# Second layer of a two-layer hybrid backbone: keys, values, queries and one convolution chunk projected ahead of the two gate chunks

## The chip, the cores and the metric

One core of one Trainium2 chip. The metric is the device time of one launch in microseconds (us); lower is better. Every time below is of the kernel as it stands, from three timed runs and one profiled execution.

## What is computed

The reference runs two layers over 256 latent tokens and 256 context tokens of width 1024. Each layer projects its normalised input with one matrix `w_in`, whose columns feed three parallel groups of heads, and then applies an output projection and a SwiGLU. Cut to what matters here:

```
proj  = h  @ p['w_in']                       # latent tokens: all columns
projc = hc @ p['w_in'][:, :n_ctx_cols]       # context, last layer: keys, values, xb and dt alone
xb = silu(dwconv(proj[xb]));  cm = silu(dwconv(proj[C]))      # state-space heads
y  = ssd_scan(xb, dt, a, bm, cm, init) + ssd_d * xs           # both directions
y_ssd = rmsnorm(y * silu(z))                                  # z: the gates
q = rope(rmsnorm(q)); k = rope(rmsnorm(k)); y_att = rmsnorm(softmax(q k') v)
y_hy  = rmsnorm(x0 * long_conv(v * x1))                       # hy: dwconv of 6 chunks
x = x + g1 * (concat(y_ssd, y_att, y_hy) @ w_out)
```

All arithmetic is float32; every product with a weight is three matmuls, of a rounded and a rest part of each side.

## The kernel before

The four instruction streams (SP for loads, TensorE, ScalarE, VectorE) are written by hand, each as a Python loop; each runs in the order in which it is written, with semaphores between them. A weight passes as pieces of 128x1024 elements through a ring of four buffers (`RING`). SP loads piece i once piece i-4 has been used (`w_used`), ScalarE rounds it (`round_w`, L1305), VectorE takes the rest (`split_w`, L1689), TensorE multiplies.

The stage "in" has 15 chunks of 256 columns, two pieces each, so 30 pieces. The list `W_IN` (L42) sets their order for both layers: four `xbc` chunks (state-space inputs), two `z` (the gates), `kv` (keys and values), two `q` (queries), six `hy` (convolution). I call piece s of the stage slot s. Work beside the projections is hung on slots by the constants of L79 to L82: in slot s TensorE runs `at_piece(s)`, then half of the piece's matmuls, then `in_piece(s)`, then the other half. In the second layer this is

- slots 7, 8, 9: transposes of x and B; slot 11 (`S_G`): the products of B and C
- slots 12 to 20 (`S_HEAD`): one state-space head a slot. TensorE spreads the sums (`cum_rows`, L805, L807), ScalarE exponentiates (L1433), VectorE adds and masks (L1947, L1948), and in the next slot TensorE makes the head's output (L818), which VectorE adds to `ysum` (L1877)
- slots 13 to 24 (`S_STATE`): the states, all through one PSUM bank `ACC` that the head outputs share. TensorE fills it in `in_piece` (L908, L914) once VectorE has read what was in it (`acc_read`)
- slots 18 to 24: queries and keys are squared (`S_SQUARES`, L1449, sums at L1974), scaled by their roots (`S_ROOTS` 20, L1460) and turned by the rotary tables (`S_ROPE` 21 to 24, L2006 to L2019), and TensorE transposes the outcome from slot 23 on (`S_TURN`)
- slots 25 to 27 (`S_GATE`): `ysum` times the silu of z, its root mean square (`token_rms`, L1288 to L1290), its scaling; slot 29 (`S_FEAT`): transposed and split (L1695)

A chunk is read out of PSUM in the even slot after it: `kv` and `q` by VectorE (L1855, L1861), `z` by ScalarE (L1378, Silu), `hy` by both (L1373, then L1838 and L1842). Two pairs of banks take turns; a `q` or `z` chunk takes both, so the chunk behind it waits until it is read out (`pair_open`).

ScalarE needs a function table for Silu and one for Ln and Exp. `preload_act_table_set("natural_log_exp_and_others")` at slot `S_HEAD` (L1425) loads one set that has Ln and Exp both. Where the program holds no such call, the build puts an `ACT_TABLE_LOAD` ahead of an activation whose function the loaded set lacks. In the stage "out" behind it, Ln and Exp come in pairs: `norm_features` for the convolution (`hrs`, ahead of the softmaxes) and for the attention (`ars`, behind them), then `norm` (L1262, L1263) ahead of the SwiGLU. The next preload is that of Silu, at L1582.

Of the kernel before, what the change touches and what calls it, by code (L numbers as in the profile page):

```python
# [30 lines left out]
CW = 256  # L31
OFF_K, OFF_XB, OFF_DT, OFF_C, OFF_Q, OFF_Z, OFF_HY = 0, 256, 1024, 1040, 1296, 1808, 2320
# [6 lines left out]
NV = NA + NB  # L39


W_IN = ([("xbc", OFF_XB + CW * i, i) for i in range(3)] + [("xbc", OFF_C, 3)]  # L42
        + [("z", OFF_Z + CW * i, i) for i in range(2)] + [("kv", OFF_K, 0)]
        + [("q", OFF_Q + CW * i, i) for i in range(2)]
        + [("hy", OFF_HY + CW * i, i) for i in (0, 2, 1, 3, 4, 5)])

FFN = [(0, 6), (6, 5)]
DOWN_ROWS = [(0, 4, 8, 12), (0, 4, 7, 10)]
# [29 lines left out]

S_DT, S_CUMS, S_XS0, S_XS1, S_B, S_G, S_HEAD, S_STATE, S_GATE, S_FEAT = 5, 6, 7, 8, 9, 11, 12, 13, 25, 29  # L79

S_SQUARES, S_ROOTS, S_ROPE, S_TURN = 18, 20, 21, 23
S_FOLD, S_TABLES = (24, 27), (20, 15)  # L82

S_TAPS, S_SUMS, S_SPEC = 6, 8, 9
# [1 line left out]
V_SINE0, V_SINE1, V_TAPS = 6, 9, 12  # L86

SMALL_LOADS, LATE_LOADS = 14, 5
CONV_CHUNKS = sum(kind in ("xbc", "hy") for kind, _, _ in W_IN)
FEAT_BANK = ((5, 6, 7, 5), (5, 6, 7, 4))  # L90


# [107 lines left out]
def backbone(nc, x, c, ctx_in, c_ctx, w_mod, b_mod, norm1_g, w_in, ssd_conv_w, ssd_conv_b, ssd_a_log,  # L200
# [3 lines left out]
    with ExitStack() as stack:  # L204
# [18 lines left out]
        xbc = at("xbc", 88, [8, T])  # L223
# [185 lines left out]
        def _(sp):  # L409
# [52 lines left out]

            def load_in(l, s):
                ch, half = in_source(s)
                kind, col, idx = W_IN[ch]
                if kind in ("z", "q"):

                    i, k0 = PLAN[l, "in"][0] + s, 4 * idx + 2 * (s % 2)
                    if i >= RING:
                        sp.wait_ge(w_used, i - RING + 1)  # L470
                    c0 = col - CW * idx
                    sp.dma_start(w_raw[:, i % RING, :].rearrange("p (k n) -> p k n", n=2 * CW),
                                 w_in[l].rearrange("(k p) n -> p k n", p=P)[:, k0:k0 + 2, c0:c0 + 2 * CW]).then_inc(w_full[i % RING], 16)
# [28 lines left out]
            for l in range(DEPTH):  # L502
# [66 lines left out]
        def _(pe):  # L569
# [169 lines left out]
            for l in range(DEPTH):  # L739
# [488 lines left out]
        def _(act):  # L1228
# [89 lines left out]
            for l in range(DEPTH):  # L1318
# [30 lines left out]
                for s in range(2, 32):  # L1349
# [4 lines left out]
                        round_w(g0 + 4)  # L1354
                        round_w(g0 + 5)
                    if ch >= 0 and s % 2 == 0:
                        kind, _, idx = W_IN[ch]
                        q = q0 + ch
                        b = 2 * (q % 2)
                        if kind in ("xbc", "hy"):  # L1360
                            act.wait_ge(w_used, g0 + max(2 * ch + 2, 4))
                            if kind == "hy" and idx == 3:
                                p.after("hyv_ready")
                            for jj in range(2):
                                blk = 2 * idx + jj
                                if kind == "xbc":
                                    wide = T if idx < 3 else n
                                    dst, wc, bc = xbc[:, blk, 0:wide], V_SCW + 8 + blk, V_SCB + blk
                                else:
                                    wide = n  # L1370
                                    dst = x1t[:, jj, 0:n] if idx in (2, 3) else (hyv, None, x0)[idx // 2][:, blk % 4, 0:n]
                                    wc, bc = V_HCW + 12 + blk, V_HCB + blk
                                A(dst, ps[:, b + jj, 0:wide], ACT.Identity, scale=vecT[:, l, wc:wc + 1],  # L1373
                                  bias=vecT[:, l, bc:bc + 1]).then_inc(conv_init, 1)
                        if kind == "z" and idx == 1:
                            act.wait_ge(w_used, g0 + 2 * ch + 2)
                            for t in range(tiles):
                                ins = A(zs[:, t, :], ps[:, 2 * ((q - 1 + t // 2) % 2) + t % 2, :], ACT.Silu)  # L1378
                                if t % 2 == 1:
                                    ins.then_inc(pair_free[(q - 1 + t // 2) % 2], 1)  # L1380
                                elif tiles == 2:
                                    ins.then_inc(pair_free[q % 2], 1)
                    if 4 <= s < 30:
                        round_w(g0 + s + 2)
                    if s % 2 == 1 and s >= 3 and W_IN[(s - 3) // 2][0] == "xbc":
                        q, idx = q0 + (s - 3) // 2, W_IN[(s - 3) // 2][2]
                        wide = T if idx < 3 else n
                        act.wait_ge(pair_free[q % 2], q // 2 + 1)
                        p.sig(A(xbc[:, 2 * idx:2 * idx + 2, 0:wide], xbc[:, 2 * idx:2 * idx + 2, 0:wide], ACT.Silu), "conv_ready")
# [46 lines left out]
                    if s == S_HEAD:  # L1436
# [2 lines left out]
                            hd = slice(h * HD, (h + 1) * HD)  # L1439
                            ins = A(ysum[:, 0:tiles, hd], xsn[:, 0:tiles, hd], ACT.Copy, scale=bc16[:, l, 2, h:h + 1])  # L1440
                        p.sig(ins, "ysum_init")
                    if s in (S_SQUARES, S_SQUARES + 1):
                        if s == S_SQUARES:
                            p.after("qk_ready")
                        for t in (2 * (s - S_SQUARES), 2 * (s - S_SQUARES) + 1):
                            if t >= 2:
                                p.after("head_ss")
                            h0 = 0 if t < tiles else 512
                            p.sig(A(hsqs[:, t % 2, h0:QKW], qk[:, t, h0:QKW], ACT.Square), "heads_squared")  # L1449
                    if s == S_HEAD + HEADS + 1:  # L1450
                        p.after("y_head_done", 2)
                    if s == S_ROOTS:
                        p.after("head_ss", 2)
                        p.chain(A(rs40[:], rs40[:], ACT.Ln, scale=1.0 / HD, bias=eps1[:, 0:1]))
                        p.chain(A(rs40[:], rs40[:], ACT.Exp, scale=-0.5))
                    if S_ROOTS <= s < S_ROOTS + 4:
                        t = s - S_ROOTS
                        for h in range(0 if t < tiles else 8, 10):
                            qh = qk[:, t, h * HD:(h + 1) * HD]
                            ins = A(qh, qh, ACT.Copy, scale=rs40[:, t, h:h + 1])  # L1460
                        p.sig(ins, "heads_scaled")
# [165 lines left out]
        def _(dve):  # L1627
# [147 lines left out]
            for l in range(DEPTH):  # L1775
# [35 lines left out]
                for s in range(2, 32):  # L1811
# [5 lines left out]
                        p.after("dt_psum")  # L1817
                        p.sig(V.tensor_copy(csT[0:32, :], ps[0:32, 6, :]), "dt_rows")
                    if ch >= 0 and s % 2 == 0:
                        kind, _, idx = W_IN[ch]  # L1820
                        q = q0 + ch
                        b = 2 * (q % 2)
                        if kind in ("xbc", "hy"):
# [125 lines left out]
                    if state_at(s) is not None:  # L1949
# [16 lines left out]
                            p.chain(TT(heads(ps[:, ACC, :]), heads(ps[:, ACC, :]), per_head(ecs, reader, d), ALU.mult))  # L1966
                            p.sig(TT(ysum[:, reader, :], ysum[:, reader, :], ps[:, ACC, :], ALU.add), "acc_read")
                        split_w(g0 + s + 2)
                    if s in (S_SQUARES, S_SQUARES + 1):
                        for t in (2 * (s - S_SQUARES), 2 * (s - S_SQUARES) + 1):  # L1970
                            h0 = 0 if t < tiles else 8
                            p.after("heads_squared")
                            p.own("qk_ready")
# [2 lines left out]
                    if s == S_TABLES[l]:  # L1976
# [342 lines left out]
```

## Time and profile before

| | |
|---|---|
| median of three runs | 1304.5 us (1302.06 to 1306.15) |
| the profiled execution | 1304.85 us |
| its span, first to last instruction | 1303.0 us, mean granted TensorE clock 0.992 |
| TensorE busy | 1241.6 us (95%) |
| VectorE busy | 700.9 us (54%) |
| ScalarE busy | 524.0 us (40%) |
| DMA | 131 GB/s over the span |

The profile gives for each engine the time in which it executed something, and for each idle stretch what ended it. Start times count from the first instruction. Instructions on one engine overlap a little (the next starts before the one ahead has ended), so what an instruction costs its queue is the distance from its start to the next one's start.

### The profile page before, as it was taken

Reading aid. Unit: us, or ns where it says so; the run is one execution under the profiler, and the core shown is the slowest. Engines: PE = TensorE matmul, PEld = TensorE weight load, DVE = VectorE, ACT = ScalarE, POOL = GpSimd, SP = SyncE. Lnnn points to the kernel's source line nnn. Section 1 sums busy time; section 2 is a strip of 40 time slices with the busy share of each in tenths; the row PEclk is TensorE's granted clock in tenths of the full one; section 3 lists DMA queues with packets and bytes.
Section 4 is the critical chain, followed back from the end, with each engine's and each line's share of the span. In section 5 each row is a group of like instructions: output and inputs, shape, how many; then the busy total and the mean of one; then the engine's idle time right before and its main releaser. Section 6 shows DMA issues by size and latency. Waiting matters only on the chain. (4 is left out here: it accounts for less than half of the span.)

```text
span 1303.0 us, 17960 instructions
## 1 busy us (share of the span) xinstructions
PE 1241.6 (95%) x7476; PEld 994.5 (76%) x7476; DVE 700.9 (54%) x1193; ACT 524.0 (40%) x902; POOL 1.7 (0%) x8
## 2 busy tenths in 40 slices
PE   5899999999999899999999999999998898999998
PEld 3566777777676677677777788768878677999998
DVE  1645256877866643432232333465479877555554
ACT  4443434542444433222112222246555354543444
POOL 0000000000000000000000000000000000000000
PEclk9899999999999999999999999999999999999999
DMA  9632344441112264455445322313334213555553
GB/s 362 216 131 97 98 145 137 139 146 49 33 39 92 65 217 150 147 177 178 162 177 178 128 93 83 107 43 95 106 98 130 90 34 98 184 188 178 183 178 126
DMA packets 129256, 171.90 MB, mean 132 GB/s; under 512 B 9204, under 2 KB 112278, under 8 KB 128152
## 3 DMA queue, kind: packets, MB, share of 16 engines
q1 hardware_dynamic: 128692, 170.58, 39.6%
q8 instruction: 59, 0.97, 0.3%
q10 hardware_dynamic: 484, 0.18, 0.1%
q14 instruction: 21, 0.17, 0.0%
HBM read 169.69 MB, written 1.05 MB: 131 GB/s over the span
## 5 line engine op out<-in xcount | busy, mean ns | idle before, releaser
L1689 DVE TENSOR_TENSOR w_lo<-w_raw,w_hi 128x1024 fp32r<-128x1024 f32 (+1 forms) x220 | 264.1, 1203 | 313.0 <-ACT w_hi L1305 312.5
L1305 ACT ACTIVATE w_hi<-w_raw 128x1024 fp32r<-128x1024 f32 (+1 forms) x220 | 228.4, 1042 | 386.3 <-DMA w_raw<-in_w_gu_dram 182.2
L654 PE MATMUL ps<-h_hi,w_hi 128*128 128x512 f32 (+1 forms) x896 | 311.9, 348 | 3.8 <-ACT gate L1597 1.8
L656 PE MATMUL ps<-h_hi,w_lo 128*128 128x512 f32 (+1 forms) x896 | 304.1, 339 | 0.0
L655 PE MATMUL ps<-h_lo,w_hi 128*128 128x512 f32 (+1 forms) x896 | 304.1, 339 | 0.0
L654 PEld LDWEIGHTS ps<-h_hi,w_hi 128*128 128x128 f32 x896 | 170.8, 191 | 38.0 <-issue 20.3
L654 PE MATMUL ps<-f_hi,w_hi 128*128 128x512 f32 (+1 forms) x544 | 187.8, 345 | 5.7 <-DVE att_lo L2205 2.7
L656 PEld LDWEIGHTS ps<-h_hi,w_lo 128*128 128x128 f32 x896 | 170.8, 191 | 19.1
L655 PEld LDWEIGHTS ps<-h_lo,w_hi 128*128 128x128 f32 x896 | 171.0, 191 | 16.9
L656 PE MATMUL ps<-f_hi,w_lo 128*128 128x512 f32 (+1 forms) x544 | 182.9, 336 | 0.0
L655 PE MATMUL ps<-f_lo,w_hi 128*128 128x512 f32 (+1 forms) x416 | 139.9, 336 | 0.0
L654 PEld LDWEIGHTS ps<-f_hi,w_hi 128*128 128x128 f32 x544 | 103.1, 190 | 23.5 <-issue 6.8
L656 PEld LDWEIGHTS ps<-f_hi,w_lo 128*128 128x128 f32 x544 | 103.1, 190 | 10.9
L655 PEld LDWEIGHTS ps<-f_lo,w_hi 128*128 128x128 f32 x416 | 78.9, 190 | 8.3 <-issue 0.5
L705 PE MATMUL ps<-h_hi,w_hi 128*128 128x512 f32 (+1 forms) x128 | 48.9, 382 | 10.8 <-DVE h_lo L1641 5.3
L2223 DVE TENSOR_TENSOR hidden<-gate,ps 128x1024 f32<-128x1024 f32 (+1 forms) x22 | 20.9, 952 | 55.7 <-PE ps L656 55.5
L706 PE MATMUL ps<-h_lo,w_hi 128*128 128x512 f32 (+1 forms) x128 | 48.3, 377 | 0.0
L707 PE MATMUL ps<-h_hi,w_lo 128*128 128x512 f32 (+1 forms) x128 | 48.0, 375 | 0.0
L1488 ACT ACTIVATE prob<-ps,sm 128x512 f32<-128x512 f32 (+1 forms) x48 | 29.1, 611 | 40.5 <-DVE sm L2098 38.0
L966 PE MATMUL ps<-w_hi,h_hi 128*128 128x512 f32 x96 | 40.5, 421 | 0.0
L705 PEld LDWEIGHTS ps<-h_hi,w_hi 128*128 128x128 f32 x128 | 25.5, 199 | 16.9 <-issue 10.7
L1433 ACT ACTIVATE em<-ps,bia 128x128 f32<-128x128 f32 x96 | 26.5, 381 | 27.9 <-PE ps L807 27.9
(301 smaller groups left out, 1580.1 us busy)
## 6 DMA issues: line engine op xcount, KB each, us to landing
w_raw<-in_w_gu_dram SPq DMA_DIRECT2D x88, 512.0 KB, 3.6
w_raw<-in_w_in_dram SPq DMA_DIRECT2D x60, 512.0 KB, 3.7
m_raw<-in_w_mod_dram SPq DMA_DIRECT2D x32, 512.0 KB, 4.7
w_raw<-in_w_down_dram SPq DMA_DIRECT2D x32, 512.0 KB, 3.4
m_even<-in_w_mod_dram SPq DMA_DIRECT2D x12, 1024.0 KB, 5.8
m_odd<-in_w_mod_dram SPq DMA_DIRECT2D x12, 1024.0 KB, 5.8
m_first<-in_w_mod_dram SPq DMA_DIRECT2D x8, 1024.0 KB, 10.8
w_raw<-in_w_out_dram SPq DMA_DIRECT2D x16, 512.0 KB, 3.4
```

The source lines that it names most:

```text
L654: mm(o, w_hi[:, i % RING, w], hi[:, 0:n], start=first and k == 0, stop=False)
L655: mm(o, w_hi[:, i % RING, w], lo[:, 0:n], start=False, stop=False)
L656: last = mm(o, w_lo[:, i % RING, w], hi[:, 0:n], start=False, stop=final and k == nk - 1)
L705: mm(o, w_hi[:, s, w], hi, start=(half == 0 and k == 0), stop=False)
L706: mm(o, w_hi[:, s, w], lo, start=False, stop=False)
L707: last = mm(o, w_lo[:, s, w], hi, start=False, stop=(half == 1 and k == 3))
L966: mm(o, h_hi[:, b, tok], w_hi[:, (i + half) % RING, w], start=(b == 0), stop=False)
L1305: A(w_hi[:, i % RING, w], w_raw[:, i % RING, w], ACT.Copy).then_inc(w_hi_done, 1)
L1433: ins = A(em[:, 2 * (h % 2) + d, t * P:(t + 1) * P], ps[:, 6 + d, t * P:(t + 1) * P], ACT.Exp, bias=bia[:, t, d * 8 + h:d * 8 + h + 1])
L1488: p.sig(A(prob[:, i % 2, j, 0:keys], ps[:, 4 + j, 0:keys], ACT.Exp, bias=sm[:, 0, c:c + 1], accum_out=sm[:, 1, c:c + 1]), "probs_ready")
L1689: TT(w_lo[:, i % RING, w], w_raw[:, i % RING, w], w_hi[:, i % RING, w].bitcast(F32), ALU.subtract).then_inc(w_lo_done, 1)
L2223: TT(hidden[:, :, 0:n], gate[:, :, 0:n], ps[:, 2 * ((q + 1) % 2):2 * ((q + 1) % 2) + 2, 0:n], ALU.mult).then_inc(pair_free[(q + 1) % 2], 1)
```

## The change

The list is now one per layer. The first layer's is the old one. In the second layer the old chunks 4 and 5 (the gates) come after the old chunk 9: four `xbc`, `kv`, two `q`, `hy` 0, two `z`, then the other five `hy`. With it the squares (slots 14, 15), the roots (slots 16 to 19) and the first two rotary steps (slots 17, 18) move forward in the second layer; the last two rotary steps stay at 23 and 24, and so do the transposes, the gate and all state-space work.

```
-W_IN = ([("xbc", OFF_XB + CW * i, i) for i in range(3)] + [("xbc", OFF_C, 3)]
-        + [("z", OFF_Z + CW * i, i) for i in range(2)] + [("kv", OFF_K, 0)]
-        + [("q", OFF_Q + CW * i, i) for i in range(2)]
-        + [("hy", OFF_HY + CW * i, i) for i in (0, 2, 1, 3, 4, 5)])
+W_IN_0 = ([("xbc", OFF_XB + CW * i, i) for i in range(3)] + [("xbc", OFF_C, 3)]
+          + [("z", OFF_Z + CW * i, i) for i in range(2)] + [("kv", OFF_K, 0)]
+          + [("q", OFF_Q + CW * i, i) for i in range(2)]
+          + [("hy", OFF_HY + CW * i, i) for i in (0, 2, 1, 3, 4, 5)])
+W_IN = [W_IN_0, [W_IN_0[i] for i in (0, 1, 2, 3, 6, 7, 8, 9, 4, 5, 10, 11, 12, 13, 14)]]
...
-S_SQUARES, S_ROOTS, S_ROPE, S_TURN = 18, 20, 21, 23
+S_SQUARES, S_ROOTS, S_ROPE, S_TURN = (18, 14), (20, 16), ((21, 22, 23, 24), (17, 18, 23, 24)), 23
...
-                    if S_ROOTS <= s < S_ROOTS + 4:
-                        t = s - S_ROOTS
+                    if S_ROOTS[l] <= s < S_ROOTS[l] + 4:
+                        t = s - S_ROOTS[l]
...
-                    if S_ROPE <= s < S_ROPE + 4:
-                        t = s - S_ROPE
+                    if s in S_ROPE[l]:
+                        t = S_ROPE[l].index(s)
```

The rest of the diff puts `W_IN[l]` for `W_IN` and `S_SQUARES[l]` for `S_SQUARES`. Line numbers of the changed kernel are one higher than those of the one before.

VectorE in slots 17 and 18 of the second layer, before (em, ysum and st are the state-space heads' tiles, w_lo the rest of a weight piece):

```order
L1877 TENSOR_TENSOR ysum<-ysum,ps 128x2x64
L1947 TENSOR_TENSOR em<-em 128x256
L1948 TENSOR_TENSOR em<-em,gT 128x256
L1955 TENSOR_TENSOR st<-st,etot 128x512
L1960 TENSOR_TENSOR st<-st,ps 128x512
L1937 TENSOR_TENSOR xw<-xsn,wst 128x512
L1689 TENSOR_TENSOR w_lo<-w_raw,w_hi 128x1024
L1861 COPY qk<-ps 128x512 x2
L1868 MEMSET rs_119 128x40
L1877 TENSOR_TENSOR ysum<-ysum,ps 128x2x64
```

The same place of the change, from slot 17's state on to the head output's addition in slot 18 (hbuf and ropt are the rotary tiles):

```order
L1956 TENSOR_TENSOR st<-st,etot 128x512
L1961 TENSOR_TENSOR st<-st,ps 128x512
L1938 TENSOR_TENSOR xw<-xsn,wst 128x512
L1690 TENSOR_TENSOR w_lo<-w_raw,w_hi 128x1024
L2007 TENSOR_TENSOR hbuf<-qk,gcos_92 128x128
L2013 TENSOR_TENSOR ropt<-qk,gsin_94 128x2x16 x4
L2007 TENSOR_TENSOR hbuf<-qk,gcos_92 128x4x64
L2013 TENSOR_TENSOR ropt<-qk,gsin_94 128x4x16 x4
L2007 TENSOR_TENSOR hbuf<-qk,gcos_92 128x4x64
L2013 TENSOR_TENSOR ropt<-qk,gsin_94 128x4x16 x4
L2020 TENSOR_TENSOR hbuf<-hbuf,ropt 128x128
L2020 TENSOR_TENSOR hbuf<-hbuf,ropt 128x4x64 x2
L1878 TENSOR_TENSOR ysum<-ysum,ps 128x2x64
```

A whole rotary step now stands between the state of slot 17 and the addition of slot 18, and a second one behind the state of slot 18; before, the read-out of the queries stood there.

ScalarE from the second layer's root mean square of `ysum` (slot 26) on, before:

```order
L1288 ACTIVATE xsn,st_117<-ysum 128x512 x2
L1289 ACTIVATE st_117<-st_117,eps_104 128x2
L1290 ACTIVATE st_117<-st_117 128x2
L1305 ACTIVATE w_hi<-w_raw 128x1024
L1373 ACTIVATE x_62<-ps,vecT 128x256 x2
```

and in the change:

```order
L1289 ACTIVATE xsn,st_117<-ysum 128x512 x2
L1290 ACT_TABLE_LOAD
L1290 ACTIVATE st_117<-st_117,eps_104 128x2
L1291 ACT_TABLE_LOAD
L1291 ACTIVATE st_117<-st_117 128x2
L1306 ACTIVATE w_hi<-w_raw 128x1024
L1374 ACTIVATE x_62<-ps,vecT 128x256 x2
```

The read-out of the gates (Silu) now comes behind the preload of slot 12, with a table load of its own ahead of it, and nothing loads the common set of Ln and Exp again: each Ln and each Exp behind it has a load. In the same way `hrs`, `ars` (L1502, L1503) and the norm's `lnt`, `rstd` (L1263, L1264) have a load each, so the second layer has nine table loads more than before: one for the gates and two for each of the four Ln and Exp pairs.

## Rows read from the trace of the kernel before

**Rows 1.** Windows: from:to, length, busy of PE, PEld, DVE, ACT, POOL, clock, DMA share, GB/s
```profile
909.13:937.74 28.61, 27.98 (x186) 24.84 (x184) 13.46 (x19) 16.96 (x33) 0.00 (x0) 1.00 0.32 95
937.74:1013.10 75.36, 66.15 (x445) 59.00 (x445) 65.42 (x155) 42.28 (x98) 0.00 (x0) 0.98 0.40 119
955.00:965.00 10.00, 8.54 (x51) 7.35 (x50) 7.33 (x13) 4.67 (x11) 0.00 (x0) 0.83 0.21 58
```

**Rows 2.** Waits of PE, 937.74 to 1013.10: us in total, times, longest us
```profile
PE ps L886 <- DVE hbuf L2019: 2.3, 2, 2.0
PE ps L914 <- DVE ysum L1877: 1.5, 2, 1.2
PE ps L914 <- DVE st L1960: 1.5, 1, 1.5
PE ps L654 <- DVE qk L1861: 1.5, 1, 1.5
```

**Rows 3.** Timeline of PE: start us, us, instruction, idle before it
```profile
909.13 1.04 PE L861 MATMUL ps<-c_sq,xbc 128*128 128x128 f32 x8
...
937.74 0.39 PE L805 MATMUL ps<-csr,pick 40*128 40x256 f32 x2
...
958.08 0.36 PE L654 MATMUL ps<-h_hi,w_hi 128*128 128x256 f32 x1 [1.46 <-DVE qk L1861]
...
1013.10 0.63 PE L1018 MATMUL ps<-c_sq,v_even 128*128 128x128 f32 x4 [1.47 <-DVE f_lo L1695]
```

**Rows 4.** Timeline of DVE, slots 17 to 22
```profile
953.56 0.68 DVE L1955 TENSOR_TENSOR st<-st,etot 128x512 f32<-128x512 f32 x1
954.31 0.69 DVE L1960 TENSOR_TENSOR st<-st,ps 128x512 f32<-128x512 f32 x1
954.91 0.69 DVE L1937 TENSOR_TENSOR xw<-xsn,wst 128x512 f32<-128x512 f32 x1
955.51 1.22 DVE L1689 TENSOR_TENSOR w_lo<-w_raw,w_hi 128x1024 fp32r<-128x1024 f32 x1
956.65 1.28 DVE L1861 COPY qk<-ps 128x512 f32<-128x512 f32 x2
...
964.63 1.54 DVE L1974 TENSOR_REDUCE rs<-hsqs 128x10 f32<-128x640 f32 x2
...
979.26 0.29 DVE L2006 TENSOR_TENSOR hbuf<-qk,gcos 128x128 f32<-128x128 f32 x1
...
982.62 0.87 DVE L1838 SCALAR_TENSOR_TENSOR x1t<-ps,vecT,x1t 128x255 f32<-128x255 f32 x2
```

**Rows 5.** Timeline of ACT, slots 7 and 20
```profile
903.83 1.04 ACT L1305 ACTIVATE w_hi<-w_raw 128x1024 fp32r<-128x1024 f32 x1
904.89 1.28 ACT L1389 ACT_TABLE_LOAD   x1
906.18 1.06 ACT L1389 ACTIVATE xbc<-xbc 128x1024 f32<-128x1024 f32 x1
...
971.49 2.49 ACT L1460 ACTIVATE qk<-qk,rs 128x64 f32<-128x64 f32 x10
```

**Rows 6.** Timeline of ACT, second layer's stage "out"
```profile
1038.62 0.47 ACT L1501 ACTIVATE hrs<-ps,eps 128x256 f32<-128x256 f32 x1 [1.22 <-PE ps L1128]
...
1040.41 0.69 ACT L1488 ACTIVATE prob<-ps,sm 128x512 f32<-128x512 f32 x1 [0.87 <-DVE sm L2098]
...
1076.40 0.47 ACT L1501 ACTIVATE ars<-ps,eps 128x256 f32<-128x256 f32 x1 [1.33 <-PE ps L1146]
...
1098.20 0.47 ACT L1262 ACTIVATE lnt<-ps,eps 128x256 f32<-128x256 f32 x1 [0.79 <-PE ps L680]
1098.70 0.42 ACT L1263 ACTIVATE rstd<-lnt 128x256 f32<-128x256 f32 x1
```

**Rows 7.** Waits of PE, 1013.1 to 1102
```profile
PE ps L705 <- DVE h_lo L1641: 2.8, 1, 2.8
...
PE ps L654 <- DVE att_lo L2205: 1.0, 1, 1.0
PE ps L680 <- ACT sqr L1255: 0.9, 1, 0.9
```

More of the change, by code:

```diff
@@ L88 @@
 SMALL_LOADS, LATE_LOADS = 14, 5
-CONV_CHUNKS = sum(kind in ("xbc", "hy") for kind, _, _ in W_IN)
+CONV_CHUNKS = sum(kind in ("xbc", "hy") for kind, _, _ in W_IN[0])
 FEAT_BANK = ((5, 6, 7, 5), (5, 6, 7, 4))
@@ L464, in load_in @@
                 ch, half = in_source(s)
-                kind, col, idx = W_IN[ch]
+                kind, col, idx = W_IN[l][ch]
                 if kind in ("z", "q"):
@@ L932, in _ @@
                 step_sizes()
-                for ch, (kind, col, idx) in enumerate(W_IN):
+                for ch, (kind, col, idx) in enumerate(W_IN[l]):
                     if ch < 2:
@@ L1356, in _ @@
                     if ch >= 0 and s % 2 == 0:
-                        kind, _, idx = W_IN[ch]
+                        kind, _, idx = W_IN[l][ch]
                         q = q0 + ch
@@ L1384, in _ @@
                         round_w(g0 + s + 2)
-                    if s % 2 == 1 and s >= 3 and W_IN[(s - 3) // 2][0] == "xbc":
-                        q, idx = q0 + (s - 3) // 2, W_IN[(s - 3) // 2][2]
+                    if s % 2 == 1 and s >= 3 and W_IN[l][(s - 3) // 2][0] == "xbc":
+                        q, idx = q0 + (s - 3) // 2, W_IN[l][(s - 3) // 2][2]
                         wide = T if idx < 3 else n
@@ L1441, in _ @@
                         p.sig(ins, "ysum_init")
-                    if s in (S_SQUARES, S_SQUARES + 1):
-                        if s == S_SQUARES:
+                    if s in (S_SQUARES[l], S_SQUARES[l] + 1):
+                        if s == S_SQUARES[l]:
                             p.after("qk_ready")
-                        for t in (2 * (s - S_SQUARES), 2 * (s - S_SQUARES) + 1):
+                        for t in (2 * (s - S_SQUARES[l]), 2 * (s - S_SQUARES[l]) + 1):
                             if t >= 2:
@@ L1451, in _ @@
                         p.after("y_head_done", 2)
-                    if s == S_ROOTS:
+                    if s == S_ROOTS[l]:
                         p.after("head_ss", 2)
@@ L1819, in _ @@
                     if ch >= 0 and s % 2 == 0:
-                        kind, _, idx = W_IN[ch]
+                        kind, _, idx = W_IN[l][ch]
                         q = q0 + ch
@@ L1968, in _ @@
                         split_w(g0 + s + 2)
-                    if s in (S_SQUARES, S_SQUARES + 1):
-                        for t in (2 * (s - S_SQUARES), 2 * (s - S_SQUARES) + 1):
+                    if s in (S_SQUARES[l], S_SQUARES[l] + 1):
+                        for t in (2 * (s - S_SQUARES[l]), 2 * (s - S_SQUARES[l]) + 1):
                             h0 = 0 if t < tiles else 8
```

## The prediction

> **What bounds the kernel now.** The page's first part comes first: TensorE is busy for 95% of the span, so only its idle time and its slow time can be won or lost. The windows then show where these lie in the stage that changes. Slots 8 to 13 (909.13 to 937.74) are TensorE's: 27.98 us busy of 28.61, with VectorE busy for 13.46 [rows 1]. From slot 14 to the first matmul of the stage behind it (937.74 to 1013.10) TensorE is busy for 66.15 us of 75.36, VectorE for 65.42 [rows 1, 3]. Two engines with equal work that hand results to each other set this stretch. TensorE idles 9.2 us in it. The waits name VectorE every time: 2.3 for the rotary tile hbuf, 1.5 and 1.5 for the bank that the states share, 1.5 for the read-out of the queries [rows 2], 1.47 for f_lo at the end [rows 3]. From 955 to 965 the granted clock is 0.83 [rows 1], close behind the 1.46 us wait of slot 18 [rows 3]. Part of that time is at 1.2 instead of 2.4 GHz, about 10 x 0.17 = 1.7 us lost.
>
> **Slots 8 to 13.** Before they hold four z pieces and two kv pieces, now two kv and four q pieces. A q piece has the matmuls of a z piece, and the transposes and first heads stay in their slots. The sum is unchanged, so slot 14 starts about 28.6 us behind slot 8 as before [rows 3]. **0.0 us**. The pieces behind kv load while the first q pieces run, as they did before; ScalarE needs the first of them 6 us earlier than TensorE, and that slack stays.
>
> **Slots 14 to the end of the stage.** TensorE has the same matmuls in another order. VectorE has 1.3 us less (the kv read-out, now in slot 10). So nothing is removed here; the question is where the waits fall. I laid out both queues from slot 14's start, each instruction at its distance in the rows: a weight rest 1.14 (955.51 to 956.65), the state's two steps and the weighing 0.75 + 0.60 + 0.60, a rotary step 3.36 (979.26 to 982.62), the two sums of squares 1.5, the q read-out 1.3 to 1.4 [rows 4], ten scaled copies on ScalarE 2.49 [rows 5].
> - Slot 14: hy 0 waits until VectorE has read q. The second head's exponentials now come late, since slots 12 and 13 are short (3.4 and 5.1 us) and ScalarE spends 1.28 on a table, 2.4 on ysum and two weight roundings ahead of them. VectorE so ends its slot 13 work about 2.5 after slot 14's start, and the read-out at 3.9. TensorE is there at 1.2 and waits 2.7; before, 1.46.
> - Slots 15 and 16: the sums of squares, the tables and hy 0's convolution put VectorE some 2 us behind, and ScalarE's scaling (2.49) holds back the exponentials of slot 17. TensorE waits about 1.2 in all.
> - Slot 18: TensorE stands at the state matmul at 23.8. The bank is free only when VectorE has added the head of slot 17, and that addition stands behind the first rotary step. VectorE does slot 17 as 0.2 + 0.8 + 0.75 + 0.6 + 0.6 + 1.14 + 3.36 = 7.5 us, with 1.75 of waiting for the exponentials, and reaches the addition at 27.2. Wait: 3.4.
> - Slot 19: the same behind the second rotary step, TensorE at 32.0, VectorE at 34.7. Wait: 2.7.
> - Slot 20: the gates are read out by ScalarE, 0.8.
> - Slots 21 to 24: with the rotary work gone VectorE keeps up, and the 2.3, 1.5 and 1.2 of before disappear.
> - Slots 26 to 29: two table loads of 1.28 [rows 5] stand in token_rms and delay the rounding of piece 29 and with it VectorE's queue by 3 us. TensorE waits 1.3 for the scaled ysum and 2.7 for f_lo.
>
> The waits add up to 2.7 + 1.2 + 3.4 + 2.7 + 0.8 + 1.3 + 2.7 = 14.8 us. The layout ends 77.3 us after slot 14's start, against 75.36: +1.9. My TensorE slots add up to 62.4, while the rows give 66.15 less 1.7 of slow clock = 64.4. If the missing 2.0 lay wholly on the path, the end would be at 79.3, +3.9. VectorE's queue sets most of the end, so I stay near the lower value and allow for a slow stretch of clock like the one before: **+2.5 us**. The bounds: all 7 us of waits that VectorE causes from slot 19 on gone and nothing new (-7); VectorE's work end to end plus all its waits of the layout and a second slow stretch (+7).
>
> **Table loads in the stage behind.** A load takes 1.28 us, starts when the instruction ahead has ended (904.87, load at 904.89) and the activation follows at 906.18 [rows 5]. A load ahead of a Ln can run while ScalarE waits for its input; the load between Ln and Exp never can.
> - hrs: 1.22 of idle covers the first load but for 0.06 [rows 6]. The second delays hrs by 1.3, to about 1040.9, where the second softmax could start at 1040.41 [rows 6]. **+0.5**; nothing, if the softmaxes catch up; 1.3, if not.
> - ars: 1.33 of idle covers the first [rows 6]. The second delays the attention's features by 1.3. TensorE already waits 1.0 for them, and then has 0.9 of slack before the squares [rows 7]. **+0.5**, between 0.4 and 1.3.
> - norm: 0.79 of idle covers 0.8 of the first 1.28 [rows 6]. The rest, 0.5, and the whole second load lie between the last square and the first matmul of the SwiGLU, which waits 2.8 already [rows 7]. **+1.8**; 1.3 at least, 2.6 if the first load waits behind the semaphore.
> - The gates' own load at slot 20 comes while ScalarE waits for TensorE: 0.
>
> The Trainium skill, "ScalarE: Activation LUTs", section "What ACT_TABLE_LOAD costs", gives a load of 1.28 us and a drain of 1.38 with it, 2.66 for a switch. Rows 5 show the 1.28 and no gap for a drain. By the page the six loads that I count as exposed would cost some 8 us more.
>
> **Sum.** 1304.85 (profiled) + 0.0 + 2.5 + 0.5 + 0.5 + 1.8 = 1310.1. The median of the runs lies 0.35 lower: **1309.8 us**, +0.4%. What a measurement of this kernel can tell from no change is about 0.3%, 3.9 us: 1300.6 to 1308.4.
>
> **The rivals.**
> - *The new waits offset the old* (same). The two queues may slide into each other better than in my layout; slots 17 and 18 cost 3 us instead of 6, the rest as above. The stage then gives -1.5 to 0, the loads +2.8: about 1305.5. For it: equal work on both engines, 10 us of idle on VectorE. Against it: the bank's order is rigid. Chance 0.30.
> - *The relief wins* (faster). The 2.3 + 1.5 + 1.2 of rotary and state waits and the 1.47 at the end go [rows 2, 3], and VectorE reaches slot 18's addition before TensorE does. It decides at 23.8 us after slot 14: VectorE would have to be 3.4 us ahead of my layout. -6.5 in the stage; of the loads the ones in norm stay, 1.8: 1304.5 - 6.5 + 1.8 = 1299.8. Chance 0.13.
> - *A table load costs twice.* If each switch also stops ScalarE for about the same time again, the four loads between Ln and Exp and the two exposed ones ahead of Ln cost 6 x 1.3 = 7.8 more, of which half a microsecond or two hides: 1309.8 + 6 = 1315.8. It is the page's drain, told as a mechanism of this kernel. Against it: rows 5. Chance 0.05.
> - *My forecast*, 1306 to 1314: chance 0.52. A part of it, about 0.05, lies below 1308.4.
>
> **How the numbers follow.** Faster by over 0.3%: 0.13. Within: 0.30 + 0.05 = 0.35. Slower: 0.47 + 0.05 = 0.52. The range 1301 to 1315 leaves out the faster rival but for its edge, and the doubled load. The forecast's own range is 1306 to 1314.
>
> **What the changed profile would show.** Slot 14 still 28.6 us behind slot 8. TensorE waiting for ysum (L1878) at the state matmuls of slots 18 and 19, 3.4 and 2.7 us; for qk at slot 14, 2.7. No wait for hbuf. Loads of 1.28 on ScalarE, nine more in the layer, and h_lo's wait ahead of the SwiGLU at 4.5 instead of 2.8. The forecast is wrong if the two rotary steps pass with under 2 us of waits, if the stretch from slot 14 to the first transposes of the stage "out" is under 74 us, or if the loads run beside idle time that I did not see.

## The result, and the profile after

| | before | after |
|---|---|---|
| median of the runs | 1303.7 us (4 runs, 1302.06 to 1306.15) | 1313.87 us (4 runs, 1312.79 to 1316.14) |
| ratio | | 1.0077 (95%: 1.0060 to 1.0095) |
| span of the profiled execution | 1303.0 us | 1312.4 us |
| mean granted TensorE clock | 0.992 | 0.987 |
| busy: TensorE, VectorE, ScalarE | 1241.6, 700.9, 524.0 | 1247.8, 701.6, 534.9 |

The change makes the kernel 0.77% slower, about 10 us. ScalarE is busy for 10.9 us more, and 9 x 1.28 = 11.5 us of table loads were added. TensorE has the same matmuls and is busy for 6.2 us more, which is already a hint: that time is clock.

I cut both spans at the same instructions. Columns of the windows: from:to, length, busy of PE, PEld, DVE, ACT, POOL, clock, DMA share, GB/s. The kernel before, slot 8 to the end of the stage "in", then the stage "out" to the SwiGLU, then the rest:

```profile
909.13:1013.10 103.97, 94.13 (x630) 83.84 (x629) 78.87 (x174) 59.24 (x131) 0.00 (x0) 0.98 0.37 113
...
1013.10:1100.91 87.81, 79.60 (x624) 65.04 (x625) 63.40 (x124) 41.39 (x87) 0.00 (x0) 1.00 0.26 78
1100.91:1303.00 202.09, 195.10 (x1612) 194.75 (x1612) 108.07 (x124) 92.05 (x116) 0.00 (x0) 0.98 0.52 167
```

The same three stretches after the change, and the two parts that answer to [rows 1]:

```profile
908.06:1016.85 108.79, 97.36 (x631) 85.27 (x629) 79.12 (x174) 62.37 (x134) 0.00 (x0) 0.95 0.38 108
...
908.06:936.93 28.87, 28.52 (x188) 24.78 (x186) 12.51 (x21) 16.94 (x32) 0.00 (x0) 1.00 0.39 110
936.93:1016.85 79.92, 68.84 (x446) 60.49 (x445) 66.61 (x154) 45.43 (x102) 0.00 (x0) 0.94 0.38 108
...
1016.85:1109.26 92.41, 81.06 (x625) 66.48 (x625) 63.53 (x124) 49.10 (x93) 0.00 (x0) 0.98 0.25 73
1109.26:1312.40 203.14, 196.19 (x1612) 195.80 (x1612) 108.43 (x124) 91.97 (x116) 0.00 (x0) 0.98 0.53 166
```

The reading that carries the rest of this document: length less busy is what TensorE waits. The number of matmuls is the same, so what busy grows by is matmuls at a lower clock. A granted clock of 1.00 is 2.4 GHz and 0.50 is 1.2 GHz: in the change the matmuls of 256 columns start 0.12 us apart at 944.6 to 945.0, and 0.21 apart at 941.0 to 942.7, where the clock is low. The clock column says the same within its rounding: 108.79 x 0.05 less 103.97 x 0.02 is 3.4 us for the first stretch.

| stretch (before to after, us) | length | of it waiting | of it busy (clock) |
|---|---|---|---|
| slot 8 to the end of "in" | +4.82 | 9.84 to 11.43: +1.6 | 94.13 to 97.36: +3.2 |
| "out" to the SwiGLU | +4.60 | 8.21 to 11.35: +3.1 | 79.60 to 81.06: +1.5 |
| the rest | +1.05 | 6.99 to 6.95: 0.0 | 195.10 to 196.19: +1.1 |

With slot 8 starting 1.07 us earlier in this execution (908.06 against 909.13) the sum is 9.4 us, the difference of the spans. Of 10.5 us behind slot 8, 4.7 are waits and 5.8 are clock.

TensorE's waits of slots 14 to 29, which answer to [rows 2, 3]:

```profile
PE ps L909 <- DVE ysum L1878: 3.2, 1, 3.2
PE ps L655 <- DVE qk L1862: 2.3, 1, 2.3
PE ps L720 <- issue: 1.8, 1, 1.8
PE ps L1019 <- DVE f_lo L1696: 1.6, 1, 1.6
PE ps L819 <- DVE em L1949: 0.8, 1, 0.8
PE ps L915 <- DVE ysum L1878: 0.5, 1, 0.5
```

and of the stage "out", which answer to [rows 7]:

```profile
PE ps L706 <- DVE h_lo L1642: 4.6, 1, 4.6
...
PE ps L655 <- DVE att_lo L2206: 2.3, 1, 2.3
...
PE ps L681 <- ACT sqr L1256: 0.5, 1, 0.5
```

The hbuf wait and the 1.5 us for st are gone. In their place stands the ysum wait at the state matmul of slot 18, and it is followed by matmuls at half clock. The timeline of TensorE shows both (start, duration, and in brackets the idle time ahead), the windows the clock:

```profile
965.73 2.04 PE L909 MATMUL ps<-xw,bnat 128*128 128x256 f32 x4 [3.23 <-DVE ysum L1878]
```

```profile
940.00:945.00 5.00, 4.44 (x21) 4.18 (x22) 1.80 (x6) 2.31 (x3) 0.00 (x0) 0.66 0.03 11
965.00:970.00 5.00, 4.27 (x10) 3.17 (x10) 4.06 (x9) 0.00 (x0) 0.00 (x0) 0.50 0.01 3
970.00:975.00 5.00, 4.50 (x20) 3.23 (x20) 4.60 (x22) 2.90 (x7) 0.00 (x0) 0.83 0.36 105
1085.00:1090.00 5.00, 3.46 (x18) 3.29 (x19) 3.96 (x8) 2.25 (x3) 0.00 (x0) 0.77 0.43 108
1110.00:1115.00 5.00, 5.00 (x26) 5.00 (x25) 4.79 (x8) 3.38 (x6) 0.00 (x0) 0.50 0.01 3
```

ScalarE's timeline for the norm, which answers to the last two lines of [rows 6]. The same pattern stands at 1004.25 (slot 26), 1041.15 (hrs) and 1079.22 (ars):

```profile
1103.97 1.28 ACT L1263 ACT_TABLE_LOAD   x1
1105.26 0.47 ACT L1263 ACTIVATE lnt<-ps,eps 128x256 f32<-128x256 f32 x1
1105.75 1.28 ACT L1264 ACT_TABLE_LOAD   x1
1107.05 0.42 ACT L1264 ACTIVATE rstd<-lnt 128x256 f32<-128x256 f32 x1
```

### The profile page after: what moved, and what is told of

It reads as the page before. It is cut to its first block and busy times, and to the rows that moved or that the text cites. A ratio compares the mean times of both kernels' runs of the same rounds, so it can differ in the third digit from the quotient of the medians.

```text
span 1312.4 us, 17971 instructions
## 1 busy us (share of the span) xinstructions
PE 1247.8 (95%) x7476; PEld 998.8 (76%) x7476; DVE 701.6 (53%) x1193; ACT 534.9 (41%) x911; POOL 2.8 (0%) x8
## 3 DMA queue, kind: packets, MB, share of 16 engines
HBM read 169.69 MB, written 1.05 MB: 130 GB/s over the span
## 5 line engine op out<-in xcount | busy, mean ns | idle before, releaser
L657 PEld LDWEIGHTS ps<-f_hi,w_lo 128*128 128x128 f32 x544 | 103.9, 191 | 10.9
## 6 DMA issues: line engine op xcount, KB each, us to landing
m_first<-in_w_mod_dram SPq DMA_DIRECT2D x8, 1024.0 KB, 10.7
```

The costliest lines, as they stand in the source:

```text
L657: last = mm(o, w_lo[:, i % RING, w], hi[:, 0:n], start=False, stop=final and k == nk - 1)
```

## Experiments

Three causes can share the 10 us: the nine table loads, the chunk order itself, and the two early rotary steps. My theory after the result was that the loads are most of it (A); the rival, that order and rotary steps are (B). Ratios below are to the kernel before, with 95% intervals; its median was 1303.7 to 1304.6 us over the series. The two right-hand columns, in us, come from each kernel's own profiled execution: TensorE's waiting from slot 8 to the SwiGLU, and how much its busy time there exceeds the 173.7 us of the kernel before (94.13 + 79.60), which is time at the lower clock.

| kernel | ratio (95%) | waiting | clock |
|---|---|---|---|
| before | 1 | 18.1 | 0 |
| after | 1.0077 (1.0060 to 1.0095) | 22.8 | +4.7 |
| e1, after + preload | 1.0020 (1.0009 to 1.0030) | 17.6 | +4.4 |
| e2, before + loads | 1.0050 (1.0036 to 1.0064) | 23.2 | +1.5 |
| e3, e1 with all steps in the old slots | 0.9998 (0.9987 to 1.0009) | 17.6 | +1.9 |
| e7, e1 with rotary in thirds | 0.9976 (0.9964 to 0.9987) | 15.5 | +1.1 |
| e10, after with rotary in thirds | 1.0050 (1.0033 to 1.0068) | 21.4 | +5.6 |

### e1: the loads taken out of the change

```diff
@@ ScalarE, read-out of the gates (slot 20 of the second layer)
+                            if l == 1:
+                                act.preload_act_table_set("natural_log_exp_and_others")
```

> The change, with one more preload of the common set of Ln and Exp behind the read-out of the gates (slot 20 of the second layer): nine added table loads become two. Theory A (most of the loss is table loads): the stage 'out' goes back from 92.4 to 87.8 us (-4.6) and the end of the stage 'in' loses the loads of slot 26 (-2), so about 1307 us, +0.3% against the kernel before. Theory B (the order and the two early rotary steps are most of it): the loads cost what their own waits show and no more (norm 1.8), so about 1312, +0.6%. By my prediction's terms: 1313.9 - 2.8 = 1311.

Measured: 1307.59 us, ratio 1.0020. The loads cost 1.0077 - 1.0020 = 0.57%, some 7.4 us of the 10. The traces say where: TensorE waits 22.8 us in the change and 17.6 here, 5.2 less. The waits of e1 that answer to those of after:

```profile
PE ps L909 <- DVE ysum L1880: 3.2, 1, 3.2
PE ps L706 <- DVE h_lo L1644: 2.8, 1, 2.8
...
PE ps L655 <- DVE att_lo L2208: 1.0, 1, 1.0
```

h_lo is back at 2.8, att_lo at 1.0, and the 1.8 us ahead of L720 is gone. Theory A. The traces locate no more than that: from slot 8 to the SwiGLU the two executions differ by 5.5 us (201.2 and 195.7), while the spans differ by 8.4. The rest lies ahead of slot 8 (908.06 and 906.59), where the kernels are the same, and behind the SwiGLU's start (203.1 and 201.7).

### e2: the same loads put into the kernel before

```diff
@@ ScalarE, slot loop of the stage "in"
+                    if l == 1 and s == 21:
+                        act.preload_act_table(ACT.Silu)
```

> The kernel before with its order untouched, and a preload of the Silu table in slot 21 of the second layer, so that each Ln and Exp behind it gets a load of its own: nine loads more, as in the change. Theory A: +5 to +7 us, about 1310. Theory B: +2 to +3 us, about 1306. By the prediction's terms +2.8: norm 1.8, hrs 0.5, ars 0.5.

Measured: 1311.52 us, ratio 1.0050, so +6.5 us with the order untouched. The added waits are those of the change, line by line: h_lo 4.6, att_lo 2.3, ysum's scaling 1.8, prob 1.0:

```profile
PE ps L705 <- DVE h_lo L1643: 4.6, 1, 4.6
...
PE ps L654 <- DVE att_lo L2207: 2.4, 2, 2.3
...
PE ps L719 <- issue: 1.8, 1, 1.8
...
PE ps L1051 <- ACT prob L1490: 1.0, 1, 1.0
```

Taken out of one kernel or put into the other, the nine loads are worth 5.1 to 5.2 us of waiting and 0.5 to 0.6% in the runs, each of these with an interval of about 0.2% either way or a little less. My prediction's 2.8 us for the stage "out" compare with 3.1 to 3.3 us of waiting there.

### e3: the chunk order alone

```diff
 (on e1)
-S_SQUARES, S_ROOTS, S_ROPE, S_TURN = (18, 14), (20, 16), ((21, 22, 23, 24), (17, 18, 23, 24)), 23
+S_SQUARES, S_ROOTS, S_ROPE, S_TURN = (18, 18), (20, 20), ((21, 22, 23, 24), (21, 22, 23, 24)), 23
```

> The change with the preload of e1, and with the squares, roots and all four rotary steps of the second layer back in slots 18, 20 and 21 to 24: only the chunk order is left of the change. If the early rotary steps cost the 3.2 us of the state matmul's wait in slot 18 and its slow clock, this is 2 to 3 us faster than e1 at that place, but the old hbuf and state waits (2.3 and 1.5) come back: about e1 or 1 us less. If the order alone costs (the read-out of q ahead of slot 14), it stays at e1.

Measured: 1303.79 us, ratio 0.9998. The order alone costs nothing that these runs can tell, and the early squares, roots and rotary steps cost the 0.2% of e1 (by the ratios 2.9 us between e1 and e3, and the two intervals just meet). Both my versions of the outcome had it too near e1. The read-out of the queries moves its wait from slot 18 to slot 14 and nothing more:

```profile
940.73 0.36 PE L655 MATMUL ps<-h_hi,w_hi 128*128 128x256 f32 x1 [1.38 <-DVE qk L1864]
...
984.12 1.13 PE L915 MATMUL ps<-st,xbc 128*128 128x256 f32 x4 [1.49 <-DVE st L1963]
988.70 0.63 PE L887 MATMUL ps<-c_sq,hbuf 128*128 128x128 f32 x4 [2.03 <-DVE hbuf L2022]
```

1.38 us for qk stands here at slot 14, against 1.46 at slot 18 before [rows 3], with the old waits for st and hbuf behind it. Note in the table that e3 and e1 wait equally long, 17.6 us each. The early steps trade 3.2 us of ysum for 2.3 of hbuf and 1.5 of st. In these two executions what they cost shows in the other column, 2.6 us of clock; e6 below tests whether the clock by itself is what is lost.

### e4: the two early steps behind the last head

```diff
 (on e1)
-((21, 22, 23, 24), (17, 18, 23, 24)), 23
+((21, 22, 23, 24), (20, 21, 23, 24)), 23
```

> The change with the preload of e1, squares and roots early as in the change, but the first two rotary steps in slots 20 and 21, behind the last of the head outputs' additions. If my account of slots 17 to 19 is right, no ysum wait of 3.2 at slot 18 and no half clock behind it, and still no hbuf wait: 3 us faster than e1, about 1303 to 1304. If VectorE's total work sets the stretch, the waits only move to slots 20 to 24 and it equals e1.

Measured: 1306.97 us, ratio 1.0016 (1.0005 to 1.0027): equal to e1, the second outcome. No 3.2 us wait at slot 18, but one of 3.66 in slot 23. There VectorE reaches the addition to st at 989.00, behind the second rotary step (982.50 to 985.8) and the convolution, and half clock follows:

```profile
989.74 0.80 PE L915 MATMUL ps<-st,xbc 128*128 128x256 f32 x1 [3.66 <-DVE st L1963]
```

```profile
990.00:995.00 5.00, 5.00 (x20) 4.64 (x21) 3.55 (x5) 0.58 (x2) 0.00 (x0) 0.50 0.00 0
```

The wait only moved, to the next small operation behind a whole step that TensorE waits for.

### e5: the loads of the stage "out" alone taken out

```diff
 (on after)
                     if s == S_GATE + 1:
                         p.after("y_gated")
                         token_rms(ysum, xsn[:, 0, :], tiles, "y_rms")
+                        if l == 1:
+                            act.preload_act_table_set("natural_log_exp_and_others")
```

> The change with one preload of the common set behind token_rms (slot 27): the two loads of slot 26 and the gates' own stay, the loads of the stage 'out' (hrs, ars, norm) go. By e1 and e2 all nine loads are worth 0.5 to 0.57% (6.6 to 7.4 us), of which their traces put 2.7 to 3.4 in slot 26 and about 3.2 to 4.6 in the stage 'out'. So 1313.9 - 3.2 to 4.6 = about 1310, +0.45% against the kernel before. If the loads of slot 26 cost nothing by themselves (my prediction counted only layout there), it equals e1: +0.2%.

Measured: 1309.29 us, ratio 1.0035 (1.0024 to 1.0047), near the first outcome. The second, e1's 1.0020, lies below this interval, but e1's own interval reaches up to 1.0030, so the loads of slot 26 alone (0.15%) can't be told from nothing by the runs. The loads of the stage "out" alone come to 1.0077 - 1.0035 = 0.42%, 5.5 us with some 2.7 either way. The place of the preload isn't free either. It stands ahead of the rounding of a weight piece, and the wait ahead of L720 grows from 1.85 to 3.26, by 1.4, which is the third load in a row:

```profile
1011.63 1.94 PE L720 MATMUL ps<-c_sq,ysum 128*128 128x128 f32 x8 [3.26 <-issue]
```

This wait isn't added whole. The wait of 1.6 us for f_lo behind it is gone, so that TensorE waits 11.0 us from slot 14 to the end of the stage, as in the change (11.1); but it is busy for 70.3 us and not 68.8, at a clock of 0.81 over 1013 to 1018, and the stretch is 81.3 us long against 79.9. Behind the gates' read-out, where e1 has its preload, no wait of this kind shows.

### e8: what one load costs in a place that nothing covers

```diff
 (on before; extra is true for the second layer's norm)
                 p.chain(A(lnt[:, 0:n], ps[:, STAT, 0:n], ACT.Ln, scale=1.0 / D, bias=eps1[:, 0:1]))
+                if extra:
+                    act.preload_act_table(ACT.Silu)
```

> The kernel before with a preload of the Silu table between Ln and Exp of the norm ahead of the second layer's SwiGLU: two loads more (Silu, and the one Exp then needs) in a place that nothing covers. If a load costs its 1.28 us and nothing with it, h_lo's wait grows by 2.56 to 5.3 and the kernel by 0.2%. If each switch also drains the engine for about as long again (2.66 in all), by 5.3 us and 0.4%. A slow stretch of the clock behind the longer wait would add up to 1 us in either case.

Measured: 1307.62 us, ratio 1.0021 (1.0009 to 1.0033). The wait for h_lo went from 2.75 to 5.32, by 2.57 us for two loads. ScalarE's timeline leaves no gap of 0.1 us between any of its four instructions:

```profile
1097.04 0.47 ACT L1262 ACTIVATE lnt<-ps,eps 128x256 f32<-128x256 f32 x1 [0.79 <-PE ps L680]
1097.53 1.28 ACT L1264 ACT_TABLE_LOAD   x1
...
1098.82 1.28 ACT L1265 ACT_TABLE_LOAD   x1
...
1100.12 0.42 ACT L1265 ACTIVATE rstd<-lnt 128x256 f32<-128x256 f32 x1
```

A load costs 1.28 us and nothing with it. The Trainium skill, "ScalarE: Activation LUTs", section "What ACT_TABLE_LOAD costs", counts a drain on top, 2.66 us for a switch; an estimate by it puts the wait at 8.1 us (2.75 + 2 x 2.66). The measured 5.32 decides against it here.

### e6: the clock of slot 18

24 matmuls whose result nothing uses, into a PSUM bank that is free in this stage, ahead of the 3.2 us wait:

```diff
 (on e1)
                             p.after("xw_ready")
+                            if l == 1 and s == 18:
+                                for k in range(24):
+                                    mm(ps[:, MOD, 0:256], h_hi[:, 4, 0:P], w_hi[:, (PLAN[l, "in"][0] + s) % RING, 0:256], start=True, stop=True)
                             p.after("acc_read")
```

> e1 with 24 extra matmuls into an unused bank at the state matmul of slot 18, just ahead of TensorE's 3.2 us wait for VectorE's addition to ysum. They produce nothing that is used; the output is the same. They take 24 x 0.12 = 2.9 us, so they fit into the wait. If the half clock from 965 to 971 follows from the idle wait, it goes, and slots 18 to 19 get 2 to 3 us shorter than e1's 10.7: total about 1305, +0.0%. If the clock falls anyway, or VectorE sets the time there, slots 18 and 19 stay at 10.7 and the total at e1.

Measured: 1306.1 us, ratio 1.0011 (1.0000 to 1.0023), which can't be told from e1's. In the trace the half clock is gone, and slots 18 and 19 begin 9.06 us apart, not 10.67. The windows 963:973 of e1 and then of e6:

```profile
963.00:973.00 10.00, 8.65 (x29) 6.29 (x30) 8.73 (x30) 2.90 (x7) 0.00 (x0) 0.67 0.19 52
```

```profile
963.00:973.00 10.00, 8.44 (x51) 6.76 (x49) 9.86 (x42) 4.79 (x12) 0.00 (x0) 1.00 0.21 60
```

But VectorE is busy for 9.86 us of those 10, and TensorE at full clock only reaches the next place sooner: it waits 2.41 us for ysum in slot 19 where e1 waits 0.55:

```profile
974.12 2.08 PE L918 MATMUL ps<-st,xbc 128*128 128x256 f32 x4 [2.41 <-DVE ysum L1883]
```

So the idle wait did bring the half clock of slot 18 (the change, e1 and e5, which all have the wait, need 10.7 us for the slot). In the trace the clock isn't what could be won there: the slot is 1.6 us shorter and the next wait 1.9 longer, since VectorE's queue stood behind it. The runs agree, but loosely: e6 gains 0.09% on e1, with 0.16% either way.

### e7: the rotary steps in thirds

```diff
 (on e1)
-S_SQUARES, S_ROOTS, S_ROPE, S_TURN = (18, 14), (20, 16), ((21, 22, 23, 24), (17, 18, 23, 24)), 23
+S_SQUARES, S_ROOTS, S_ROPE, S_TURN = (18, 14), (20, 16), ((21, 22, 23, 24), (17, 18, 19, 20, 21, 22, 23, 24)), 23
+S_ROPE_AT = ([(t, None) for t in range(4)], [(t, k) for t in range(2) for k in range(3)] + [(2, None), (3, None)])
...
+                        if third is not None:
+                            parts = parts[third:third + 1]
```

> e1 with the two early rotary steps cut into thirds of about 1.1 us each, one third a slot in slots 17 to 22, the same VectorE work (but more semaphore waits of its own). If the price of the early steps is that a whole one (3.4 us) stands ahead of an addition that TensorE waits for, the 3.2 us wait falls under 1 and its slow clock goes, and hbuf's 2.3 does not come back: 3 to 5 us faster than e1, about 1303 or -0.1%. If VectorE's sum of work sets the stretch, no gain over e1.

Measured: 1300.55 us, ratio 0.9976: 0.44% faster than e1 and faster than the kernel before, by 3 to 4 us. VectorE does the same arithmetic. The wait of slot 18 is 0.80, with no slow clock behind it, hbuf has no wait, and st 0.3:

```profile
961.46 1.10 PE L910 MATMUL ps<-xw,bnat 128*128 128x256 f32 x4 [0.80 <-DVE ysum L1881]
966.75 1.13 PE L916 MATMUL ps<-st,xbc 128*128 128x256 f32 x4 [0.33 <-DVE ysum L1881]
...
984.46 1.13 PE L916 MATMUL ps<-st,xbc 128*128 128x256 f32 x4 [0.32 <-DVE st L1964]
```

So VectorE's sum of work doesn't set the stretch. How much of a rotary step stands in one slot does: e4 and e11 move the whole steps to other places and stay near e1. (The thirds are also spread over six slots; thirds one right behind the other would be a whole step again.)

### e11: the same two steps whole, but behind the addition

In e11 VectorE adds to ysum first in slots 18 and 19 and then does the whole rotary step, ahead of em and the state.

```diff
 (on e1; the step's code is now a function)
-S_SQUARES, S_ROOTS, S_ROPE, S_TURN = (18, 14), (20, 16), ((21, 22, 23, 24), (17, 18, 23, 24)), 23
+S_SQUARES, S_ROOTS, S_ROPE, S_TURN = (18, 14), (20, 16), ((21, 22, 23, 24), (18, 19, 23, 24)), 23
...
+                    if l == 1 and s in (18, 19):
+                        rotary(s)
                     if 4 <= s < 30 and state_at(s) is None:
                         split_w(g0 + s + 2)
```

> e1 with the two whole early rotary steps (3.4 us each) moved from the end of slots 17 and 18 to behind the addition to ysum in slots 18 and 19: the same pieces of work, not cut, the addition first. If only the addition behind the step was the trouble, the 3.2 us wait goes and the total comes near e7, about 1301 to 1302. If a step of 3.4 us hurts wherever it stands in a slot of 3.9 to 5 us, TensorE waits instead for em of slots 18 and 19 or for the state behind it, 2 to 3 us: about e1, 1307.

Measured: 1305.11 us, ratio 1.0011 (0.9993 to 1.0029), not to be told from e1 and 0.35% slower than e7, with about 0.2% either way. The trace shows the second outcome in smaller size: 2.35 us for what stands behind the first step and 1.49 behind the second, at the heads of the next slots:

```profile
966.36 0.65 PE L819 MATMUL ps<-xsn,em 128*128 128x64 f32 x4 [2.35 <-DVE st L1998]
973.79 0.63 PE L819 MATMUL ps<-xsn,em 128*128 128x64 f32 x4 [1.49 <-DVE ysum L2005]
```

### e10 and e9: adding up, and a miss

e10 is e7 without e1's preload, so the change with the thirds and all its loads.

```diff
 (on e7)
-                            if l == 1:
-                                act.preload_act_table_set("natural_log_exp_and_others")
```

> The change with the rotary thirds of e7 alone, without the preload, so all nine added table loads stay. If the two causes add up, it costs what the loads cost in e1 and e2, +0.5 to +0.57% more than e7: about 1307.5 to 1308.5, +0.3% against the kernel before. If the loads matter less once TensorE has fewer waits beside them, or more, it lies outside 1306 to 1310.

Measured: 1309.31 us, ratio 1.0050 (1.0033 to 1.0068). The step from e7 is 0.74%, 9.6 us, with an interval of about 0.2% either way; its lower end, 0.53%, lies between the 0.57% and 0.50% of e1 and e2. The two causes add up within what can be told. Its profiled execution (1313.37 us, one of its slowest) has four slow stretches where e7 has two. TensorE waits 21.4 us in it and 15.5 in e7, 5.9 more; 0.9 of that is the wait for the queries in slot 14 (2.3 against 1.4), ahead of which the kernels have the same instructions.

e9 moves ScalarE's start of ysum in the second layer from slot 12 to slot 10.

```diff
 (on e7)
-                    if s == S_HEAD:
+                    if s == (S_HEAD, 10)[l]:
                         p.own("xsn_ready")
```

> e7 (rotary in thirds, one more preload) with ScalarE's start of ysum, eight scaled copies of 2.4 us in all, moved in the second layer from slot 12 to slot 10, where ScalarE idles. In e7 TensorE waits 0.8 for ScalarE's em and 1.0 for VectorE's em in slots 12 to 17 and is at half clock for part of 930 to 940. If ScalarE's work in slot 12 causes these, slots 12 to 14 get 1 to 2.5 us shorter: about 1299, -0.35%. If VectorE's read-out of the queries in slot 14 sets the time there, that wait grows by what the others lose: equal to e7, -0.24%.

Measured: 1302.11 us, ratio 0.9984 (0.9970 to 0.9998), no better than e7. In its trace 930 to 940 is at full clock and slot 14 starts 29.5 us behind slot 8 and not 31.3, but TensorE still waits 0.8 for ScalarE in slot 12, now for gT, and 1.4 for qk. The early slot 14 isn't the doing of the move: e4, e6 and e10, which don't have it, start slot 14 at 29.3 to 29.7. From slot 8 to the SwiGLU its execution takes 188.7 us and e7's 190.3; the runs don't confirm that gain. The best version found is e7.

## Why the prediction was right, and where it was not

Forecast 1309.8 us, slower by 0.4%; measured 1313.87, slower by 0.77%. It is in the direction given the largest chance, at the upper edge of the forecast's own range (1306 to 1314), and the loss is nearly twice the forecast one. Step by step:

- **Slots 8 to 13: 0.0.** Measured +0.26 (28.61 to 28.87). Right in this execution. In e1, e3 and e7, which have the same instructions there, the stretch is 31.1 to 31.3 us, with a slow stretch of clock in it; then slot 14 is shorter (6.4 us instead of 9.1). In e4, e6 and e10 it is 29.3 to 29.7. From slot 8 to slot 15 all kernels with the new order but e9 (35.9) take 37.5 to 39.9 us against 33.3 before. With the steps in their old slots (e3) this comes back: slots 15 to 18 take 17.3 us instead of 21.1, for the wait for the queries is no longer in slot 18. The change has its first rotary step there and doesn't get it back: from slot 8 to slot 19 it takes 62.2 us, e3 54.7 and the kernel before 54.4. From slot 19 to the end of the stage it takes 46.6 against 49.6, the relief.
- **Slot 14, queries: 2.7.** Measured 2.3, with slow clock behind it.
- **Slots 15 to 17: 1.2. Slot 20, the gates: 0.8.** Measured 0.8, for em in slot 17, and in slot 20 0.4, for a weight rest and not for the gates.
- **Slot 18, ysum behind the first rotary step: 3.4.** Measured 3.23. The mechanism and its size were right, the size with some luck: TensorE was ready 25.6 us after slot 14's start and VectorE began the addition at 28.4, where the layout had 23.8 and 27.2.
- **Slot 19: 2.7.** Measured 0.5. TensorE was at half clock through slot 18 and so came late itself (ready 36.5 us after slot 14's start and not 32.0; the addition began at 36.7 and not 34.7). When e6 kept its clock up the wait was there, 2.41. I had laid TensorE's slots out at full clock behind a wait that I knew to be 3.4.
- **Slots 21 to 24: the waits for hbuf and st gone.** They are.
- **Slots 26 to 29: ysum 1.3, f_lo 2.7.** Measured 1.8 and 1.6.
- **The stretch from slot 14: +2.5.** Measured +4.56. This term was mis-sized. Against my layout TensorE waited less, 79.92 - 68.84 = 11.1 us instead of 14.8, and was busy longer, 68.84 instead of 62.4. Of these 6.4 us 5 are low clock (below), and the other 1.4 are matmul time that my layout lacked; I knew that up to 2.0 were missing and left most of them out of the path. Set beside the kernel before, waiting grew by 1.9 us and busy time by 2.7. I allowed for "a slow stretch of clock like the one before"; 940 to 945 and 965 to 975 are three times that: 5 x (0.34 + 0.50 + 0.17) = 5 us against 1.7.
- **hrs: +0.5.** Measured +0.4 (prob waits 1.0, before 0.6). **Norm: +1.8.** Measured 4.56 - 2.75 = 1.81, and by e8 two uncovered loads give 2.57. **The gates' own load: 0.** ScalarE idles 2.29 us behind it.
- **ars: +0.5.** The wait for att_lo grew by 1.28, of which a third came back at the squares (0.87 to 0.54), so +0.95 of waiting, inside my 0.4 to 1.3. But 1085 to 1095 then ran at 0.77 and 0.89, 1.7 us more. e2 has the same wait of 2.29 and full clock behind it.
- **Behind the SwiGLU's start: nothing foreseen.** Measured +1.05. The first 20 us are at 0.86 instead of 0.91, behind a longer wait.
- **The loads of the stage "out" together: +2.8.** By e5 they cost 5.5 us in the runs, give or take 2.7. The added waiting there was 3.1, near what I had. In the traced execution TensorE was also busy for 1.5 us more in the stage and 1.1 behind it, at the lower clock, and I had put no clock into these terms.

The forecast's sign came from the right causes, but its balance was not quite that of the chip. In my layout the waits behind the loads of slot 26 (1.3 and 2.7, against 1.5 before) alone were as large as the whole +2.5, which leaves order and rotary steps near nothing. By e1 to e3 the loads cost 6.5 to 7.4 us, the chunk order 0, the early rotary steps nearly 3. "A table load costs twice" (1315.8) lay nearer to the measured time than my forecast and is false as a mechanism: e8 shows 1.28 for each. "The relief wins" named what is to be had, and e7 collects a part of it once the steps are cut.

What stays open: why a slow stretch follows one wait and not another of the same length (att_lo, 2.29 us, in the change and in e2), and so how much of the 5.8 us of clock a further execution would show in the same places. Thirds of a rotary step within the old chunk order weren't tried, since the roots there come in slot 20 and leave no slots to spread them over.

## What to carry to other kernels

When the only caller of a shared function table goes ahead of a function from another table, look at everything behind it: the build puts a load ahead of each Ln and each Exp, and one preload in a slot where ScalarE idles took back 0.57% here. When a block of work is moved earlier on a busy in-order engine, ask what small operation now stands behind it; the same VectorE work in thirds, one a slot, turned +0.20% into -0.24%. And in a sum made against a trace, keep waits and clock apart (length less busy, and busy against busy): a wait that is added can come back as a slow stretch and hide the next wait.

## What the runs showed that I had not expected

The same instructions do not get their slow clock in the same place. e8 is the kernel before up to its norm, yet in its profiled execution 955 to 965 is at full clock, and 985 to 995 and 1020 to 1030 are not; in the kernel before it is the other way round. The kernel before, then e8 (e8 runs some 3 us earlier, 906.15 against 909.13 at slot 8):

```profile
985.00:995.00 10.00, 6.48 (x47) 6.07 (x47) 9.86 (x30) 3.74 (x6) 0.00 (x0) 1.00 0.24 73
1020.00:1030.00 10.00, 8.22 (x68) 7.85 (x68) 7.89 (x13) 2.12 (x2) 0.00 (x0) 1.00 0.35 110
```

```profile
955.00:965.00 10.00, 9.04 (x64) 8.18 (x65) 8.33 (x17) 4.26 (x10) 0.00 (x0) 1.00 0.30 92
985.00:995.00 10.00, 8.13 (x53) 7.99 (x54) 9.39 (x24) 3.94 (x7) 0.00 (x0) 0.83 0.28 71
1020.00:1030.00 10.00, 8.21 (x57) 8.01 (x56) 5.25 (x9) 2.72 (x3) 0.00 (x0) 0.83 0.38 122
```

A window of 10 us at 0.83 costs 10 x 0.17 = 1.7 us. Two executions of one instruction stream can so differ by 1.7 us at a given slot, and agree again a few slots later where VectorE had been behind. For differences under some 3 us the busy column of a single trace is therefore weak evidence, while the waiting column repeats better: the loads were worth 5.1, 5.2 and 5.9 us in three pairs of kernels, and 0.9 of the last is the wait for the queries in slot 14, which is 1.4 us in some executions and 2.3 in others of the same instructions up to there. The Trainium skill, "TensorE: Matmul & The Clock Gate", section "Part 1: The HAM clock gate", states of the slow matmuls at a kernel's start that their number varies from run to run of one kernel. The rows above show slow stretches in the middle of a kernel that differ between executions.

The second surprise is that filling a wait with matmuls worked on the clock, from 0.67 to 1.00 over 963 to 973, and bought next to nothing (0.09%, within the error of 0.16%).
